# Seven half-size products in place of eight for the projections of a differential attention phase

## The reference, cut to what matters

```python
def project(u, n):
    q, k, v, z = jnp.split(u @ w_in, 4, axis=-1)      # w_in: 1024 x 8192
    q = rms_norm(q.reshape(bsz, n, 2 * DIFF_HEADS, DIFF_DH), qn_g)
    k = rms_norm(k.reshape(bsz, n, 2 * DIFF_HEADS, DIFF_DH), kn_g)
    v = v.reshape(bsz, n, DIFF_HEADS, DIFF_VDH)
    return q, k, v, z
# q_l, k_l of the 512 tokens are rotated; keys and values are tokens' and context's together
s = jnp.einsum('bqnd,bknd->bnqk', q, k).astype(F32) * scale
p = jax.nn.softmax(s, axis=-1)
w = p[:, :, 0] - lam * p[:, :, 1]                     # two softmaxes a head
o = jnp.einsum('bhqk,bkhe->bqhe', w, v)
o = rms_norm(o, subln_g) * (1.0 - lam_init)
out = (o.reshape(bsz, n, D_INNER) * jax.nn.silu(z)) @ w_out
```

## Time and profile before

| | |
|---|---|
| runs (us) | 3730.9, 3731.12, 3731.86; median 3731.12 |
| the profiled execution | 3729.2 us, its span 3727.4 us |
| TensorE busy | 3590.8 us (96%) |
| VectorE busy | 1863.5 us (50%) |
| ScalarE busy | 1183.2 us (32%) |
| GpSimd busy | 308.0 us (8%) |
| mean granted clock of TensorE | 0.987 |
| the differential phase | from 1575 us to 2672 us of the span |

### The profile page before, as it was taken

How to read it: one execution, slowest core, us unless ns; L and a number is a source line. 1 busy time by engine, 2 the same in 40 slices (tenths; PEclk the granted TensorE clock), 3 DMA queues, 4 the chain that set the end, 5 groups by cost and what they waited for, 6 DMA issues and landing times.

```text
span 3727.4 us, 48282 instructions
## 1 busy us (share of the span) xinstructions
PE 3590.8 (96%) x17514; PEld 2489.7 (67%) x17514; DVE 1863.5 (50%) x3821; ACT 1183.2 (32%) x2199; POOL 308.0 (8%) x355
## 2 busy tenths in 40 slices
PE   8999999998999999899999999999897999999999
PEld 4455688874547888666666666666455888888864
DVE  5734643545637445434545445454304666666651
ACT  3113210112433011124444434344202555555540
POOL 6700000000000000000000000000001222222210
PEclk9999999999999999999999999999998999999999
DMA  8532434331124432411110101101011222222211
GB/s 175 149 85 60 110 94 116 88 104 28 36 64 107 108 103 79 120 35 34 34 34 28 34 28 34 34 28 34 29 51 48 63 62 61 57 58 61 62 48 62
DMA packets 455589, 246.46 MB, mean 66 GB/s; under 512 B 43280, under 2 KB 447504, under 8 KB 455472
## 3 DMA queue, kind: packets, MB, share of 16 engines
q1 hardware_dynamic: 440144, 215.79, 21.6%
q0 software_dynamic: 14144, 28.36, 2.8%
q10 hardware_dynamic: 1184, 0.71, 0.1%
HBM read 229.96 MB, written 14.80 MB: 66 GB/s over the span
## 4 chain that ended last, share of the span: by engine, by line
PE 90%; DVE 6%; ACT 2%; issue 1%; DMA 1%; SPq 0%; DVEq 0%; ACTq 0%
PE bank L557 20%; PE bank L1872 13%; PE bank L401 10%; PE bank L2424 10%; PE bank L1858 5%; PE bank L1315 3%; PE bank L1140 3%; PE bank L2443 3%; PE bank L1895 2%; PE bank L963 2%; PE bank L1189 2%; PE bank L1210 2%; PE bank L1840 2%; PE bank L940 1%; PE bank L1882 1%
## 5 line engine op out<-in xcount | busy, mean ns | idle before, releaser
L1872 PE MATMUL bank<-hT,ring 128*128 128x512 f32 x1504 | 510.5, 491 | 1.0 <-ACT arena L2075 1.0
L1872 PEld LDWEIGHTS bank<-hT,ring 128*128 128x128 f32 x1504 | 278.7, 190 | 218.8 <-issue 204.9
L401 PE MATMUL bank<-big,ring 128*128 128x512 f32 (+1 forms) x1024 | 394.1, 542 | 1.1 <-DVE big L2201 1.1
L401 PEld LDWEIGHTS bank<-big,ring 128*128 128x128 f32 x1024 | 192.4, 191 | 179.5 <-issue 171.4
L2474 POOL TENSOR_TENSOR tb<-ring 128x512 f32<-128x512 f32 x32 | 40.7, 1271 | 2810.6 <-DVE big L2951 2647.8
L1196 ACT ACTIVATE arena<-bank 128x512 f32<-128x512 f32 (+2 forms) x224 | 118.4, 529 | 408.2 <-PE bank L1189 407.3
L557 PE MATMUL bank<-big,arena 128*128 128x256 f32 x1024 | 228.8, 379 | 0.0
L557 PEld LDWEIGHTS bank<-big,arena 128*128 128x128 f32 x1024 | 194.6, 190 | 26.5
L2102 DVE TENSOR_REDUCE cols<-bank 128x1 f32<-128x768 f32 x128 | 116.5, 952 | 149.0 <-PE bank L1840 148.9
L1858 PEld LDWEIGHTS bank<-ring,hT 128*128 128x128 f32 x1536 | 175.2, 192 | 12.5 <-issue 12.5
L1858 PE MATMUL bank<-ring,hT 128*128 128x128 f32 x1536 | 178.3, 276 | 0.0
(11 more groups left out here) (343 smaller groups left out, 6099.7 us busy)
## 6 DMA issues: line engine op xcount, KB each, us to landing
ring<-in_mlp_w SPq DMA_DIRECT2D x128, 512.0 KB, 5.5
ring<-in_a_w_in SPq DMA_DIRECT2D x64, 512.0 KB, 4.0
ring<-in_b_w_in SPq DMA_DIRECT2D x64, 512.0 KB, 4.2
ring<-in_mod_w SPq DMA_DIRECT2D x48, 512.0 KB, 5.1
ring<-in_even_w_in SPq DMA_DIRECT2D x32, 512.0 KB, 4.7
bias_d<-tb POOLq DMA_DIRECT2D x96, 128.0 KB, 3.5
big<-bias_d POOLq DMA_DIRECT2D x16, 768.0 KB, 5.3
ring<-in_a_w_out SPq DMA_DIRECT2D x16, 512.0 KB, 3.9
```

The source lines that it names most:

```text
L401: mm = pe.matmul(bk(self.bank(n, j))[:, 0:z - a], ring[s][:, k % KT, :], self.rhs(k, a, z), start=k == order[0], stop=k == order[-1], skip ...
L1872: mm = pe.matmul(flatb[2][:, a:z], ring[s][:, k, :], hT[:, k, a:z], start=k == 0, stop=k == KT - 1)
```

## The change

The 512 token columns of a pair of projections (q and k; v and z) are computed as a 2 x 2 block product: two halves of the features by two halves of the tokens, and two output tiles. Instead of eight products of half size there are seven (P1 to P7), each four matmuls of 256 columns, on sums of weights (S1 to S4) and sums of data (T1 to T4):

- Data sums are made once for the phase, by `dve_sums` on VectorE, into slots 4 to 6 of the ring and into `hT` itself. Weight sums are made per head and pair on GpSimd (`pool_dif`, four operations a pair, eight a step) in slot 7. The weights have slots 0 to 3 alone, one head deep.
- The context's 256 columns are made plainly, two projections together in a bank (`context(0)`: q and k; `context(1)`: v and z). In the opening step both come first.
- ScalarE copies P1 and P5 out (`copied`), VectorE makes five evacuations of 256 columns a pair (`sum2`, `first_half`, `last_half`, `second_tile`) and copies q and k of the context (`context_qk`).
- v now comes out as the others do, so its raw values are turned by six transposes at the next step (`values`, both on TensorE and ScalarE), through bank 3.
- The order of the step is new on all three engines. SP waits for the last P7 before it loads the output weights. TensorE waits for `md_c` at 11 instead of 12, and `dve_rotk` comes after the sums.

```diff
-                ("dif", range(8), 8), ("wout2", range(8), 2),
+                ("dif", range(4), 16), ("wout2", range(8), 2),
...
+        STEP = ["Tc'", "T0", "T1", "so'", "vt", "T2", "bo'", "rq", "T3", "sq", "rk", "sk", "bk"]
...
+        class Two:
+            def __init__(self, r, first):
+                b = [bk(first + r), bk(first + 1 - r)]
+                self.C, self.X, self.Y, self.Z = b[0][:, 0:H], b[0][:, H:S], b[1][:, 0:H], b[1][:, H:S]
+        dtwo = [Two(0, 4), Two(1, 4)]
+        NPROD = {P1: ("A11", B11, "C"), P5: (S1, T1, "Y"), P6: (S2, T2, "X"), P4: ("A22", T4, "Z"),
+                 P2: ("A12", B21, "C"), P3: (S4, B22, "Y"), P7: (S3, T3, "X")}
...
+                    if x == P6:
+                        pe.wait_ge(m_copied, dth("copied", 4, g, 2 * r + 1))
+                    if x == P4:
+                        pe.wait_ge(m_copied, dth("copied", 4, g, 2 * r + 2))
+                    if x == P2:
+                        pe.wait_ge(m_u2, dth("u2", 2, g, r + 1))
+                    if x == P7:
+                        pe.wait_ge(m_c11, dth("c11", 2, g, r + 1))
```

The new functions on VectorE and GpSimd:

```diff
+            def sum2(r):
+                dve.wait_ge(m_prod, dth("prod", 14, g, 7 * r + P6))
+                dve.wait_ge(m_copied, dth("copied", 4, g, 2 * r + 1))
+                dve.wait_ge(m_c2, dth("c2", 2, g, r))
+                dve.tensor_tensor(du, dp1, w.X, ALU.add).then_inc(m_u2, 1)
...
+            def second_tile(r):
+                dve.wait_ge(m_prod, dth("prod", 14, g, 7 * r + P7))
+                dve.tensor_tensor(du, dp1, w.X, ALU.add).then_inc(m_u3, 1)
+                dve.tensor_tensor(dst_[:, 0:H], du, w.Z, ALU.subtract).then_inc(m_free, 1)
+                dve.tensor_tensor(dst_[:, H:S], du, dp5, ALU.add).then_inc(m_c2, 1)
...
+            def context_qk():
+                    multiplied(dve, "dif", 1, g)
+                b = ctx_bank(h, 0)
+                dve.tensor_copy(d_q[:, S:TT], b[:, 0:C])
+                dve.tensor_copy(d_raw[:, S:TT], b[:, C:2 * C]).then_inc(ds["gf"], 1)
...
+                        i0, i1, op = {S1: (block(b, 0), block(b, 4), ALU.add),
+                                      S2: (dsum[S1], block(a, 0), ALU.subtract),
+                                      S4: (block(a, 4), dsum[S2], ALU.subtract),
+                                      S3: (block(a, 0), block(b, 0), ALU.subtract)}[x]
+                        pool.tensor_tensor(dsum[x], i0, i1, op).then_inc(m_wsum, 1)
```

More of the change, by code:

```diff
@@ new lines, in context @@
+            def context(r):
+                if h is None:
+                    pe.wait_ge(u_c, KT)
+                else:
+                    pe.wait_ge(m_u3, dth("u3", 2, g, r + 1))
+                for j in range(2):
+                    if h is None:
+                        arrived(pe, "dif", 2 * r + j, g)
+                    for k in range(KT):
+                        mm = pe.matmul(ctx_bank(h, r)[:, C * j:C * j + C], ring[2 * r + j][:, k, :], hT[:, k, S:TT],
+                                       start=j == 0 and k == 0, stop=k == KT - 1, skip_group_check=True)
+                    if h is not None:
+                        mm.then_inc(slab_done[2 * r + j], 1)
@@ L1877, in turn, with values @@
+            def values():
+                st.n_free(pe, "vt")
+                pe.wait_ge(m_c12, dth("c12", 2, h, 2))
+                pe.wait_ge(m_b, dth("b", 1, h, 1))
+                for t in range(6):
+                    mm = pe.transpose(flatb[3][:, P * t:P * t + P], v_raw[:, P * t:P * t + P], ident)
+                mm.then_inc(m_plus, 1)
             def turn(t, x, h):
@@ L1951, in pe_dif @@
                 turn(0, "T0", h)
-            if not make:
+            if make:
+                products(0, P1, P5, P6, P4)
+            else:
                 st.g_done(pe, "pv'")
-            ahead(0, 3)
-            if make:
-                project(0, "q", 0, 4 if old else 8)
-            if old:
-                stats("so'", st.sq["o'"], ones[:, 0:32])
-            if make and old:
-                project(0, "q", 4, 8)
+                ahead(0, 3)
             if on:
@@ L1963, in pe_dif @@
                 scores(2)
-            ahead(3, 3)
             if make:
-                rotate_q()
-                project(1, "k", 0, 2)
+                products(0, P2, P3, P7)
+            else:
+                ahead(3, 3)
+            if old:
+                stats("so'", st.sq["o'"], ones[:, 0:32])
+            if on:
+                values()
+                turn(2, "T2", h)
+                scores(3)
             if old:
@@ L1970, in pe_dif @@
             if make:
-                project(1, "k", 2, 5)
-                stats_q()
-                project(1, "k", 5, 8)
-            if on:
-                turn(2, "T2", h)
-                scores(3)
-            ahead(6, 3)
-            if make:
-                rotate_k()
-                project(2, "v", 0, 2)
-                stats("sk", st.sq["k"], b64[:, 48:80])
-                project(2, "v", 2, 6)
+                rotate_q()
+                if on:
+                    context(0)
+                products(1, P1)
+            else:
+                ahead(6, 3)
             if on:
@@ L1986, in pe_dif @@
             if make:
-                project(3, "z", 0, 2)
+                stats_q()
+                rotate_k()
+                products(1, P5, P6, P4, P2)
+                stats("sk", st.sq["k"], b64[:, 48:80])
+                products(1, P3, P7)
                 broadcast("bk", st.rr["k"])
-                project(3, "z", 2, 8)
+                if on:
+                    context(1)
             else:
@@ L2049, in act_dif @@
             if on:
-                exps(1)
+                turned(1, h)
+                exps(2)
             if old:
```

295 lines of the change are left out of this document (191 added, 104 removed).

## The result

The changed kernel takes 4043.44 us (median of 4 runs, 4041.64 to 4046.4), beside 3731.47 us for the kernel before on the same chip: a ratio of 1.084 (95% interval 1.0827 to 1.0853), 312 us slower. The forecast was 3966 us with a range to 4025: the sign holds and so do the waits, the price of the lower clock behind them does not, and the time lies outside the range.

What follows compares the result with a forecast made beforehand. The prediction took the phase as TensorE-bound. Fourteen steps +185, first step +9, head -15, GpSimd +13 and clock +45 gave +237 on 3729.2 us: 3966 us, range 3870 to 4025.

Steps and rivals of the forecast that it cites:

- Matmul saving, 3.5 us a step: On TensorE, pure matmul time of projections and transposes falls from 42.7 to 39.2 us a step, saving 3.5.
- The waits, 16.7 a step: The new order makes TensorE wait for VectorE's and ScalarE's queues, 16.7 us a step in sum.
- The walk: Following one step through each engine's in-order queue to find TensorE's waits; net of saving, +13.2 us a step.
- turn(2) +2.5: At turn(2), TensorE waits for probs(2), queued behind second_tile(0) on VectorE, which waits for P7: +2.5 us a step.
- GpSimd, 0.9 a step: GpSimd's weight sums slow VectorE operations on the path: 0.9 us a step, 13 in all, bounds 0 and 2.
- Clock, 3.0 a step: After waits, TensorE's clock falls twice a step at about 1.5 us each: 3.0 a step, 45 in all.
- First full step, +9: The first step (h = 0), having neither pv' nor y_normed, becomes 9 us slower.
- Head -15: At the phase's opening, both contexts run first and fill TensorE's idle time, so first scores end 15 us earlier.
- Tail 0 ± 3: The last step (h = 15) keeps its old chain of softmax waits: 0 us, between -3 and +3.
- Rival 1: In the step, waits stay hidden and the matmul time is gained: 3660 us, chance 0.07.
- Rival 2: The step's waits are overcounted: half and no falls, 3790 us; two thirds and one fall, 3860; chance 0.12.
- Rival 3: TensorE stays at half clock for a third of a step's matmul time, 20 us a step: about 4220, chance 0.05.

Runs made afterwards that it cites:

- e1: Changed kernel with probs(3) and the read of the rotated queries put ahead of context_qk and the rest of rotated_q on VectorE: 3960.13 us.
- e7: Changed kernel with GpSimd's eight weight sums after the first head cut to 16 of 512 columns each: 4011.46 us.
- e6: e4 with probs(3) put back behind context_qk and rotated_q on VectorE, so turn(3) waits again: 3754.87 us.
- e2: Changed kernel with root_q put ahead of exps(4) on ScalarE: 4014.03 us.
- e4: Changed kernel with the order on TensorE, ScalarE and VectorE written anew, same products, sums and slots: 3683.33 us.
- e8: e4 with probs(2) also put ahead of last_half(0) on VectorE: 3679.77 us.
- e9: e8 with the second pair's first GpSimd weight sum started after the first pair's P7 instead of P3: 3666.68 us.
- e5: Changed kernel with both probs(3) ahead of context_qk on VectorE and root_q ahead of exps(4) on ScalarE: 3886.68 us.
- e3: Changed kernel with 19 dummy matmuls a pipelined step on TensorE, filling three of its waits: 3979.43 us.

## Why the prediction was wrong, step by step

- **Matmul saving, 3.5 us a step**: 3.3 (65.3 less 62.0). Right.
- **The waits, 16.7 a step**: with narrow sums, so without GpSimd's part, 15.1 less the old 0.3 = 14.8. The walk was 1.9 too high, and right in kind: six of its seven places are in the list under the cause it gave. Turn(3) +4.0: 3.74. turn(1) +1.1: 1.4. rotate_q +2.6: 2.1. pv' +1.2 over 0.3: 1.54 in all. P7 +0.8: 0.38. rotate_k +4.4: 3.2, since behind turn(3)'s wait scores(4) and `stats_q` ran slowly, which covered part of it (in e1, where they ran at full clock, it is 3.8). **turn(2) +2.5 has the right size (2.96) under another name.** The chain of the walk is in the trace as reckoned: `probs(2)` behind `second_tile(0)` ended at 2081.36, 3.7 after P7. But it wasn't last. `root(so')` on ScalarE kept `values` waiting for 2.06 and so turn(2) 0.9 more, to 2082.04, and that the second chain came out only 0.7 later than the first is luck. The walk took this root as done in time; it has no term for its table load, which starts only when the statistics are there:

```profile
2078.22 1.28 ACT L2123 ACT_TABLE_LOAD   x1 [1.79 <-PE bank L1985]
2079.51 0.42 ACT L2123 ACTIVATE tb<-bank,cst 128x192 f32<-128x192 f32 x1
```

  (start, duration, idle before: the load stands behind TensorE's statistics, and the root behind the load.)
- **GpSimd, 0.9 a step, bounds 0 to 2**: 2.3 in e7 (87.73 less 85.46), 1.5 of it waits and 0.7 the rest (which is inside the clock's 9.2 below); 32 us of the kernel where 13 stood. Mis-sized and misplaced: the forecast looked at `probs(1)` and at the evacuation ahead of `probs(2)`; the dear place was `probs(4)`, where a two-column scaling and two products were held up, and which context(1) follows: the forecast gave that wait 0.1, it is 1.25.
- **Clock, 3.0 a step, bounds 0 to 6: the step that failed.** It is 9.2 us. The number of falls was the smaller mistake: 3 stretches a step where two were taken, within the four of the bound, 1.5 of the 6.2 us that were missing. The price was the larger: 1.5 us each, read from waits that stood alone, and e6 has 1.8 there. In the changed kernel a stretch lasts 7.2 us on average, the one behind turn(3) mostly 13.7, and costs 3.1. Over fourteen steps that is 9.15 x 14 = 128 us where 42 stood, and the upper bound was taken from the same lone price. Whether the waits close together or the blocks between them made the stretches long stays open (e2, e6). The range's upper end is also added up a little low: 3729 with 179, 30 and 90 is 4028, not 4025; the measured time is outside either.
- **First full step, +9**, with the clock's 3.0 and GpSimd's 0.9 about 13: 17.9, short for the same reason.
- **Head -15**: -13.1, measured from the start of the block before it to the start of the first scores. Right within 2 us. The last block ahead of the phase and the first scores, before:

```profile
1564.78 0.38 PE L1676 MATMUL bank<-cst,tb 128*128 128x128 f32 x2
...
1628.28 1.56 PE L1840 MATMUL bank<-arena 64*128 64x512 f32 x8
```

  After, with the phase's first matmuls, which answer to the first of the earlier trace rows:

```profile
1570.85 0.38 PE L1676 MATMUL bank<-cst,tb 128*128 128x128 f32 x2
1572.16 14.05 PE L1941 MATMUL bank<-hT,ring 128*128 128x256 f32 x64 [0.94 <-DVE gsc L1725]
...
1621.26 2.93 PE L1874 MATMUL bank<-arena 64*128 64x512 f32 x8 [3.20 <-issue]
```

  The 10.17 us of idle time are 0.94. But L1676, which nothing of the change touches, starts at 1570.85 where it had started at 1564.78 before; so the first scores start only 7.0 us earlier. The opening of the phase shifts by itself from profile to profile (the first matmuls stand at 1572.63 in e4 and 1568.72 in e8, with equal code up to there). But L1676 starts at 1567.4 or later in all ten experiments too, so whether the 6.1 are the change's in part isn't shown. The first scores have 3.20 us of idle time ahead of them, for which the profile names no releaser, and ran at half clock (2.93 for 1.56); by their ends, which is how the forecast put it, the gain is 11.7.
- **Tail 0 ± 3**: -5.6. Better than said, by 2.6 beyond the bound.

From the forecast's +237 to the measured +313 are 76 us: the clock +86, GpSimd's waits +9 (1.5 a step less 0.9), the walk -27, the matmul saving +3, the first and last of the fourteen steps, which were shorter than the others, -3, the first full step +5, the head +2, the tail -6, and the 6 from before the phase.

**The rivals.** Rival 1 (the waits are hidden) is false of this order and true of another: its condition, `probs(3)` and `root_q` reached as early as before, is part of what e4 builds, and e9 (3667) comes within 7 us of its 3660. The condition alone is not enough: e5 meets it and is at 3887, since the other waits stay. Rival 2 (overcounting) has its part in the 1.9 of the waits, none in the sign; its second sum is off too, two thirds of the waits and one fall come to +122, not +130. Rival 3 (half clock for a third of the matmul time) named the right mechanism: the record has half clock in 21.5 of 87.7 us, a quarter of the step. Its price of 20 us a step was twice what it came to, and the range should have reached toward it, instead of ending at four lone falls. The argument against it, that the clock rose again after 4.29 us of idle time in the head, was drawn from a wait that stood alone.

## What to carry to other kernels

When TensorE bounds a stage, waits of 1 to 4 us close together cost more than themselves, here half as much again (9.2 us on 16.6). Don't price the half clock by a count of lone falls. In the changed kernel and in e2 it reached from the wait to the first long run of matmuls behind it, and that stretch is the better first guess; it was read from these two traces and not tried by itself. Saved matmuls paid here only when every in-order queue beside TensorE had its urgent reader (`probs`, the roots) ahead of the work that the change adds; moving it there turned +8.4% into -1.7% with the same products and sums. And a small sum on GpSimd is not free because its engine idles: see which VectorE operation starts beside it, and give it a wait that puts it elsewhere.

## What the runs showed of the hardware that was not expected

- More work can take less time: 8.2 us a step of matmuls whose results nobody reads made the kernel 64 us faster (e3), by keeping TensorE busy through three waits. The waits fell by less than the dummies took, so the gain is the clock.
- One wait of 3.05 us a step is enough for a fall of the granted clock in 12 of 13 steps (e6). The Trainium skill (TensorE: Matmul & The Clock Gate, section "Terms") reckons the penalty as the time at the lower clock times one less the ratio, so half: by that page's rule 21.5 us would cost 10.8 and e6's 3.2 would cost 1.6. The rests of the table give 9.2 and 1.7, so the trace agrees for e6, and for the changed kernel once the idle part of the stretches is left out (17.2 us busy, half of which is 8.6). The price per us was not the surprise, but how long the lower clock lasts.
- The same kind of wait was followed by 3.4 us of half clock in e6 and by 13.7 us in e2, with nearly the same idle time (3.05 and 3.74 us) in front.
- Two-column operations are held up too: 0.85 us for a scaling of 128 x 2 beside GpSimd, 0.23 without it. And starting an operation earlier under a running sum gains nothing: in e4 and e8 the scaling ended 0.4 us after the sum, whether it had started 0.62 or 0.06 us behind the sum's start.
- The table load on ScalarE (1.28 us) ahead of `root(so')` started only with the event that the root itself waits for, so it stood on the path although ScalarE had been idle for 1.79 us.
